# A smaller first weight slab, an earlier table load, and a convolution split between ScalarE and VectorE

## What is computed

```python
def ssd_mixer(u, in_w, conv_w, conv_b, dt_bias, a_log, ...):   # u = rms_norm(x), 256 x 1024
    proj = u @ in_w                       # 2048 columns z, 4096 columns xbc, 32 columns dt
    z, xbc, dt_raw = split(proj)
    xbc = silu(causal_depthwise_conv(xbc, conv_w, conv_b))     # 4 taps, each channel alone
    xs, b_in, c_out = split(xbc)
    dt = softplus(dt_raw + dt_bias)
    y = ssd_chunked(xs * dt, dt * -exp(a_log), b_in, c_out) + d_skip * xs
    y = gated_group_rms_norm(y, z, norm_w)
    return y @ out_w
```

## Time and profile before

| | us |
|---|---|
| three runs | 887.01, 890.19, 890.44 |
| median | 890.19 |
| the profiled execution | 888.14 |
| span of its trace | 886.4 |

### The profile page before, as it was taken

The page is one execution under the profiler, slowest core; times in us unless marked ns, Lnnn a source line. Parts: engine busy times, 40 slices in busy tenths (PEclk is TensorE's granted clock), DMA queues, the critical chain, the costliest instruction groups (busy, mean ns, idle before and its releaser), DMA issues.

```text
span 886.4 us, 18328 instructions
## 1 busy us (share of the span) xinstructions
PE 859.8 (97%) x7073; PEld 825.8 (93%) x7073; DVE 561.0 (63%) x1541; ACT 486.5 (55%) x923; POOL 628.4 (71%) x282
## 2 busy tenths in 40 slices
PE   8999999999999999999999999879999999999996
PEld 8999988889998899999999988768999999999996
DVE  5997758764343487776369988654556666641164
ACT  6754476655446555655645567645554444554351
POOL 3999656656986456554978998342877888889681
PEclk9999999999999999999999999989999999999998
DMA  9677633323765334342757576232555666667611
GB/s 332 197 220 214 182 116 86 106 87 105 223 192 163 101 114 147 113 146 65 220 169 213 153 224 182 87 95 73 167 170 175 188 183 185 184 189 217 189 48 48
DMA packets 38678, 138.85 MB, mean 157 GB/s; under 512 B 4416, under 2 KB 4416, under 8 KB 38592
## 3 DMA queue, kind: packets, MB, share of 16 engines
q1 hardware_dynamic: 38592, 137.69, 51.3%
HBM read 136.63 MB, written 1.05 MB: 155 GB/s over the span
## 4 chain that ended last, share of the span: by engine, by line
PE 74%; DVE 5%; POOL 4%; ACT 3%; issue 2%; POOLq 0%; ACTq 0%; DVEq 0%
PE ps L610 20%; PE ps L612 20%; PE ps L611 20%; POOL wl L556 4%; PE ps L830 1%; ACT wh L1095 1%; PE ps L738 1%; PE ps L637 1%; PE ps L655 1%; PE ps L988 1%; PE ps L961 1%; PE ps L854 1%; PE ps L826 1%; PE ps L803 1%; PE ps L720 1%
## 5 line engine op out<-in xcount | busy, mean ns | idle before, releaser
L556 POOL TENSOR_TENSOR wl<-raw,wh 128x1024 fp32r<-128x1024 f32 x254 | 611.2, 2432 | 216.3 <-ACT wh L1095 216.3
L610 PE MATMUL ps<-uh,wh 128*128 128x256 f32 x1248 | 353.1, 283 | 3.7 <-DVE wl L1612 1.5
L612 PE MATMUL ps<-uh,wl 128*128 128x256 f32 x1248 | 349.6, 280 | 0.0
L611 PE MATMUL ps<-ul,wh 128*128 128x256 f32 x1248 | 349.1, 280 | 0.0
L1095 ACT ACTIVATE wh<-raw 128x1024 fp32r<-128x1024 f32 x256 | 264.6, 1054 | 85.4 <-PE ps L612 79.8
L610 PEld LDWEIGHTS ps<-uh,wh 128*128 128x128 f32 x1248 | 234.7, 188 | 5.5 <-issue 2.0
L611 PEld LDWEIGHTS ps<-ul,wh 128*128 128x128 f32 x1248 | 235.2, 188 | 0.0
L612 PEld LDWEIGHTS ps<-uh,wl 128*128 128x128 f32 x1248 | 234.9, 188 | 0.0
L1766 DVE TENSOR_TENSOR h<-ps,h 128x256 f32<-128x256 f32 x32 | 13.6, 424 | 106.3 <-PE ps L612 106.2
L612 PE MATMUL ps<-ffh,wl 128*128 128x256 f32 x176 | 49.3, 280 | 0.0
L610 PE MATMUL ps<-ffh,wh 128*128 128x256 f32 x176 | 49.1, 279 | 0.0
(11 more groups left out here) (361 smaller groups left out, 1740.8 us busy)
## 6 DMA issues: line engine op xcount, KB each, us to landing
raw<-slabs SPq DMA_DIRECT2D x256, 512.0 KB, 4.0
h<-x_fm SPq DMA_DIRECT2D x4, 256.0 KB, 5.6
out_fm<-outb SPq DMA_DIRECT2D x4, 256.0 KB, 2.2
cst<-shape_consts SPq DMA_DIRECT2D x1, 768.0 KB, 9.1
vec<-vectors SPq DMA_DIRECT2D x1, 299.5 KB, 9.2
pin<-p_fm SPq DMA_DIRECT2D x1, 256.0 KB, 4.2
vec<-vectors SPq DMA_DIRECT2D x1, 4.0 KB, 2.4
```

The source lines that it names most:

```text
L556: nc.gpsimd.tensor_tensor(wl[:, s % PART_RING, :], raw[:, s % RAW_RING, :], wh[:, s % PART_RING, :].bitcast(f32), ALU.subtract).then_inc(s ...
L610: nc.tensor.matmul(res, w_h, a_h, start=first, stop=False)
L611: nc.tensor.matmul(res, w_h, a_l, start=False, stop=False)
L612: ins = nc.tensor.matmul(res, w_l, a_h, start=False, stop=last)
```

## The change

- **First slab.** The blocks of slab 0 hold 32 columns instead of 128, packed together: 128 partitions x 256 values (128 KB), at the head of each partition's 4 KB. SP, ScalarE and VectorE handle only these. TensorE's 24 matmuls of `dt` use 32 weight columns and write 32 partitions.
- **Table load.** A one-column ScalarE copy, waited for, stands ahead of the wait for `x`. ScalarE's first activation, before which the function table is loaded, is then this one.
- **Convolution.** The first tap of each tile is a ScalarE copy with a column as scale, `ssm_first`, for both tiles of a pair when `c` is odd, behind the split of the slab and ahead of the two SiLUs. It waits for VectorE's take of the tile. VectorE makes the other three taps, of the pair before the one that it has just taken, and those of the last pair behind the loop. The count per pair that others wait for falls from eight to six.

```diff
+DT_COLS = 32
@@ sync
-                sp_.dma_start(raw[:, s % RAW_RING, :], slabs_dram[s]).then_inc(sem(f"slab_in{s % RAW_RING}"), 16)
+                n = slab_cols(s)      # BLK * DT_COLS for slab 0, else SLAB
+                sp_.dma_start(raw[:, s % RAW_RING, 0:n], slabs_dram[s][:, 0:n]).then_inc(sem(f"slab_in{s % RAW_RING}"), 16)
@@ tensor, project_part
-                n_cols = j.wide * P
+                width = DT_COLS if name == "dt" else P
+                n_cols = j.wide * width
...
-                    c = (b % BLK) * P
+                    c = (b % BLK) * width
...
-                            res = o[:, 0:a_h.shape[-1]]
+                            res = o[0:width, 0:a_h.shape[-1]]
@@ scalar, feed_slabs
-                    nc.scalar.activation(wh[:, s % PART_RING, :], raw[:, s % RAW_RING, :], ACT.Copy)\
+                    n = slab_cols(s)
+                    nc.scalar.activation(wh[:, s % PART_RING, 0:n], raw[:, s % RAW_RING, 0:n], ACT.Copy)\
                         .then_inc(sem("wh_ready"), 1)
@@ scalar
+            act.wait_ge(sem("memset"), 2)
+            link(nc.scalar.activation(sq[:, KD - 1, 0:1], ones[:, 0:1], ACT.Copy))
             act.wait_ge(sem("gain_in"), 16)
             high(n_ssm, 0)
             high(n_ssm, 1)
@@ scalar
             def ssm_silu(c):
 
-                act.wait_ge(sem("ssm_tap"), 2 * SSM_TAPS * (c // 2 + 1))
+                act.wait_ge(sem("ssm_tap"), 2 * (SSM_TAPS - 1) * (c // 2 + 1))
...
+            def ssm_first(c):
+
+                act.wait_ge(sem("dve_evac"), freed[jobs[f"xbc{c}"].out][1])
+                wait(act, "ssm_silu", c - 3)
+                nc.scalar.activation(ssm_acc(c), sraw[:, c % 4, 0:T], ACT.Copy, scale=v("sconv_w", c * SSM_TAPS))\
+                    .then_inc(sem("ssm_first"), 1)
+
             for c in range(SSM_CT):
                 feed(f"xbc{c}")
+                if c % 2:
+                    ssm_first(c - 1)
+                    ssm_first(c)
                 if c % 2 and c > 1:
                     ssm_silu(c - 3)
                     ssm_silu(c - 2)
@@ vector, first_slab
-                tt(wl[:, s, :], raw[:, s, :], wh[:, s, :].bitcast(f32), ALU.subtract).then_inc(sem("wl_ready"), 1)
+                n = slab_cols(s)
+                tt(wl[:, s, 0:n], raw[:, s, 0:n], wh[:, s, 0:n].bitcast(f32), ALU.subtract).then_inc(sem("wl_ready"), 1)
@@ vector
             def take_xbc(c):
                 if c >= 4:
-                    dve.wait_ge(sem("ssm_tap"), 2 * SSM_TAPS * ((c - 4) // 2 + 1))
+                    dve.wait_ge(sem("ssm_tap"), 2 * (SSM_TAPS - 1) * ((c - 4) // 2 + 1))
...
             def ssm_conv(c):
 
-                wait(dve, "ssm_silu", c - 2)
-                for i in range(SSM_TAPS):
+                for i in range(1, SSM_TAPS):
                     for e in range(2):
-                        if i == 0:
-                            taken(f"xbc{c + e}")
+                        if i == 1:
+                            dve.wait_ge(sem("ssm_first"), c + 2)
                         else:
-                            dve.wait_ge(sem("ssm_tap"), SSM_TAPS * c + 2 * i + e - 1)
-                        tap(ssm_acc(c + e), sraw[:, (c + e) % 4, i:i + T], v("sconv_w", (c + e) * SSM_TAPS + i), i == 0)\
+                            dve.wait_ge(sem("ssm_tap"), (SSM_TAPS - 1) * c + 2 * (i - 2) + e + 1)
+                        tap(ssm_acc(c + e), sraw[:, (c + e) % 4, i:i + T], v("sconv_w", (c + e) * SSM_TAPS + i), False)\
                             .then_inc(sem("ssm_tap"), 1)
 
             for c in range(0, SSM_CT, 2):
                 take_xbc(c)
                 take_xbc(c + 1)
-                ssm_conv(c)
+                if c:
+                    ssm_conv(c - 2)
...
+            ssm_conv(SSM_CT - 2)
```

More of the change, by code:

```diff
@@ L515, in gain, with slab_cols @@
             return v(name, at + k)
+        def slab_cols(s):
+            return BLK * DT_COLS if s == 0 else SLAB
         block = ctx.enter_context(nc.Block())
@@ L2222, in pack_weights @@
             stream[j.at[k]:j.at[k] + j.wide] = blocks[k * j.wide:(k + 1) * j.wide]
-    return np.ascontiguousarray(stream.reshape(n_slabs, BLK, P, P).transpose(0, 2, 1, 3).reshape(n_slabs, P, SLAB))
+    slabs = stream.reshape(n_slabs, BLK, P, P).transpose(0, 2, 1, 3).reshape(n_slabs, P, SLAB)
+    slabs[0, :, 0:BLK * DT_COLS] = stream[0:BLK, :, 0:DT_COLS].transpose(1, 0, 2).reshape(P, BLK * DT_COLS)
+    return np.ascontiguousarray(slabs)
 def pack_vectors(inputs):
```

## The result

| | before | after |
|---|---|---|
| median, us | 888.52 | 890.69 |
| lowest to highest of 20 runs each | 885.1 to 891.84 | 888.41 to 893.79 |
| ratio, with its 95% interval | | 1.0024 (1.0013 to 1.0036) |
| profiled execution, and its span | 888.14, 886.4 | 890.82, 889.0 |
| mean granted clock of the profiled execution | 0.989 | 0.985 |

The changed kernel is slower by some 2.2 us, a quarter of a percent, so within the half percent that I called no change. With twenty runs each the interval still leaves out 1: far less than half a percent can be told apart. First the whole span of the kernel after: busy time and share of each engine.

What follows compares the result with a forecast made beforehand. TensorE was taken to bound the kernel, so only its waits near the edits count. 888.14 - 1.2 + 1.6 + 1.3 = 889.8, plus 1.1 for the mean of runs, gave 890.9 us; range 886.8 to 893.3.

Steps and rivals of the forecast that it cites:

- Start: Before xbc0: smaller slab 0 lands the second x piece earlier, so TensorE starts sooner, -1.2 us (-0.4 to -1.5).
- my two rates: DMA at the start: 393 kB less saves 1.5 us at 262 GB/s or 0.93 us at 422 GB/s.
- A price by rows: DMA of slab 0: if rows cost nearly the same whatever their length, the saving is only about 0.4 us.
- the start does not get what it says: Rival at the start: gain 0.4 us or less; time 890.4 us, with the clock 891.7; chance 0.12.
- cap: Start: dt, behind the warm-up products, can't end before 11.5 us, so the gain is at most 1.7 us.
- Table load: ScalarE's start: the 1.28 us load moves into the wait for x and by itself adds 0.
- The middle: Convolution, 20 to 105 us: work moved from VectorE to ScalarE makes TensorE wait for neither, counted 0.
- ScalarE becomes the pace: Rival in the convolution: a pair takes 6.6 us instead of 5.65; 897.4 us before start and tail; chance 0.04.
- Last pair: End of the convolution: twelve taps, not eight, behind the last take delay SiLUs and TensorE, +1.6 us (+1.3 to +1.9).
- Clock: Near 112 us: a 2.35 us wait halves TensorE's clock during sz1, +1.3 us if it falls; forecast with it 0.46.
- the clock stays up: Rival behind the last pair's wait: TensorE's clock does not fall; time 889.6 us; chance 0.31.
- Base: Whole kernel: three runs of before average 1.1 us above the profiled 888.14, so 1.1 us is added.

Runs made afterwards that it cites:

- e2: The kernel before with the convolution's part of the change alone, slab 0 whole and table load behind x: ratio to before 1.0024.
- e9: The kernel before with small matmuls of ones in four later TensorE waits of the attention part: median 882.39 us, ratio to before 0.9927.
- e6: The changed kernel without the tiny copy that loads the table ahead of x: one run, no interval; expected ratio 1.0011 from its trace.
- e1: The kernel before with the small first slab and early table load, its convolution untouched: ratio to before 0.9985.
- e3: The changed kernel with VectorE's taps of the former pair put between the two takes of a pair: ratio to before 0.9977.
- e5: The changed kernel with ten small matmuls of ones filling TensorE's wait behind sz0: ratio to before 1.0010.
- filled kernels: Kernels with small matmuls of ones put into four later TensorE waits of the attention part: ratios to before 0.9907 to 0.9939.
- e11: The kernel of e4_again with small matmuls of ones in four later TensorE waits: median 881.05 us, ratio to before 0.9907.
- e10: The changed kernel with small matmuls of ones in four later TensorE waits, its wait near 108 us unfilled: 884.13 us, ratio to before 0.9939.
- e4_again: Second run of before plus small first slab and early table load, tile 30's four taps made before tile 31 is taken: ratio to before 0.9988.

## Why the prediction was right, and where not

It gave 890.9, and 890.69 was measured. The agreement to 0.2 us is partly luck; step by step:

- **Start, -1.2 (-0.4 to -1.5): -1.03 measured.** The mechanism was right: the second `x` piece lands earlier and the chain of 5.7 us behind it stays. 393 kB less made it land 1.0 us earlier in this pair of executions, which is 393 GB/s, between my two rates and nearer the quick one (422). One pair says little, since the landing itself scatters by 1.1 us. But with the whole slab `xbc0` starts at 13.13, 13.18 and 13.50 (e2, before, e9), and in the ten executions with the small one and the squares in place at 11.74 to 12.74, 12.18 in the mean: 1.09 us less, and no overlap. A price by rows would have given 0.4 us; rows of 1 KB cost about by their bytes. The Trainium skill, "DMA: Bandwidth & Descriptors", section Specifications, gives 512 B as the smallest transfer for full rate; the trace agrees, with these 1.0 to 1.1 us for rows of 1 KB. The rival *the start does not get what it says* falls. One reading in the working was wrong: `dt` is not held to 8.64 us by the warm-up products. They took 7.56 us in before and 7.14 in after, where `dt` started at 7.97, so the end of `dt` is no fixed cap.
- **Table load, 0: right.** ScalarE waits 1.54 us for `x` behind slab 0 (after), and with the load at its old place still 0.72 us (e6, one execution, in which the piece landed late).
- **The middle, 0: right.** No wait for `wl` between 20 and 122 us, though slab 6 had 0.36 us of slack, and e1's mark is to a hundredth that of before. VectorE's 12.3 us less and ScalarE's 13 us more (12.7 and 11.0 by the page) are nowhere on the path. The rival *ScalarE becomes the pace* falls. ScalarE's first tap is 0.48 us and VectorE waits once for one, 1.02 us, at the first pair.
- **Last pair, +1.6 (+1.3 to +1.9): +1.58.** Twelve taps at 0.39 us pitch end 5.13 us behind the take in place of 3.55. e3 shows it by moving one line. The wait at L723, though, is 2.06 us and not 2.35. I added the 1.58 to the old wait of 0.77 and forgot that `decay_pair` also has a first half, for the SiLUs of the pair before. These are later too now (they end at 108.09), and TensorE's first two products wait for them from the end of `sz0` at about 107.87 to 108.14: 0.3 us of the wait lie there. The sum is the same, only in two pieces.
- **Clock, +1.3 if it falls: it fell, for +0.78 (e5) or +0.79 (e6).** This is the term that was mis-sized. That it falls behind a wait between 1.93 and 2.87 us was right in three of four executions. Its raw price was right as well, 4.43 - 2.93 = 1.5 us of `sz1`. But I took "a part" of the 0.34 us of the `mb` wait for all that can hide it, 0.2 to 0.4 us, where 0.72 were hidden: I had read one bracket, and not the distance from the end of `sz1` to the product with `acp`. I had also overlooked a wait in before's trace. The rival *the clock stays up* says that there is none between 1.47 and 1.93 us; but ahead of L975, at 572.98, TensorE waits 1.67 us for ScalarE's `npT`, and the clock is 1.00 from there to 576 us.
- **Base.** I put before at 889.2, the mean of three runs; twenty give 888.5. This 0.7 us too much made up for most of what I had too little: the sum's change was +1.7, by the medians it is +2.17, by the marks +1.33, with the clock held +1.74.

What I took as the whole account, 888.14 - 1.2 + 1.6 + 1.3 = 889.8, is 1.0 us below the profiled execution of after (890.82). That last microsecond is none of my steps: between 542 and 573 us after falls back by another 1.6 us (1.19 to 2.79), and that is the clock of that one execution (0.08 lower over 22 us makes 1.8). The +2.17 of the medians over the marks' 1.33 is also more than I can place. The interval of the ratio reaches down to 1.2 us, so it may be nothing. It may also be that after gets a lower clock in more of its executions. The mean granted clock of its 20 runs is 0.9870. That of before's 20 is not on record; 86 other executions of before have 0.9909, but most of them were also faster (four medians, 887.4, 887.2, 887.5 and 889.5). From their times (next section), the 888.5 us of before's 20 answer to about 0.9897, an estimate. The fall at 112 us itself (1.7 us at half the clock) is 0.002 of 888, most of that difference. Whether the rest belongs to the change stays open, as does whether the race near 400 us, below, strikes it more often.

## What to carry to other kernels

When a step is put one round behind in a loop, the middle costs nothing and the bill comes at the last round: count what is queued behind the last dependence there, and give that round an order of its own (e3 does it with one line). A gap on the bounding engine costs its length and, if it is near 2 us, more behind it; products of ones into a bank that is started anew cost nothing in a wait that has to be there (e5 goes on as far behind `xbc0` as after, 98.55 us to the product with `acp`), and in the attention part they were worth more than either half of the change. For a change of one or two microseconds compare distances between two instructions of the trace, which repeated to a few hundredths (in e6 to a tenth), before the times, which scatter by several.

## What the runs showed of the hardware

- **The time of an execution follows its mean granted clock.** Of 86 executions of before, beside which the experiments ran, the larger groups are: 889.7 us at 0.987 (mean of 7), 888.9 at 0.989 (24), 887.8 at 0.991 (15), 885.5 at 0.993 (21); the extremes are 891.7 at 0.985 and 882.8 at 0.998, one each. A line through all 86 falls by 0.7 us per 0.001 and takes up two thirds of the variance; at 0.989 alone the times still run from 886.8 to 890.9. The filled kernels have 0.993 to 0.998. Two of them scatter less than before (e9 2.0 us from lowest to highest, e11 2.4), but e10 has 4.9, near the 5.2 of before beside it.
- **Whether the clock falls behind a given wait is not fixed.** Behind 2.06 us it fell in three of four executions, and behind the same 0.80 us near 546 us the stretch has 0.84, 0.92 or 1.00. In e11 it fell there with no wait at all. I had read the trace as if the length of the wait decided.
- **The same DMA lands up to 1.1 us apart.** The second `x` piece, 256 KB issued at about the same time with the same queue ahead of it, took 3.8 to 4.9 us over the eleven executions with the small slab. At the start this is as much as the change wins.
- **A VectorE instruction can take six times its length beside one of GpSimd.** `ogl` and `mzb` have all their operands in SBUF and take 0.41 and 0.42 us alone. In before, between 300 and 408 us, 18 of these 32 instructions take longer, up to 2.65 us, and every one of the 18 ends 0.27 to 0.29 us behind the end of a GpSimd `wl` that ran beside it; so do the 18 in after and in e4_again. GpSimd is held up too: near 400 us in before its first `wl` takes 2.70 us, in e4_again 2.39. Which engine holds which there hangs on hundredths of a microsecond. In twelve of the fourteen profiles both `ogl` get through and only `mzb` is held; here is before:

```profile
399.45 0.75 DVE L1830 TENSOR_TENSOR ogl<-ogt,ogh 128x256 fp32r<-128x256 f32 x2
399.76 5.21 POOL L556 TENSOR_TENSOR wl<-raw,wh 128x1024 fp32r<-128x1024 f32 x2 [4.58 <-ACT wh L1095]
400.12 2.62 DVE L1865 SCALAR_TENSOR_TENSOR mzb<-mze,mzb 128x256 f32<-128x256 f32 x1
```

In e4_again and e10 the second `ogl` is held for the first `wl` and `mzb` for the second, and TensorE waits some 2.5 us in place of 0.3, with the clock at 0.51 and 0.52 in 2 us behind it. This is e4_again:

```profile
397.68 2.97 DVE L1857 TENSOR_TENSOR ogl<-ogt,ogh 128x256 fp32r<-128x256 f32 x2
397.98 4.88 POOL L562 TENSOR_TENSOR wl<-raw,wh 128x1024 fp32r<-128x1024 f32 x2 [4.58 <-ACT wh L1103]
400.57 2.57 DVE L1892 SCALAR_TENSOR_TENSOR mzb<-mze,mzb 128x256 f32<-128x256 f32 x1
...
404.09 1.22 PE L861 MATMUL ps<-pT,vn 128*128 128x256 f32 x2 [2.48 <-ACT pT L1286]
```

That fits with e10's profiled execution (887.25 us) being the slowest of its six. No run moves the two engines apart to test it.
